# The gate tiles of attention in a two-block transformer kernel, with two of their three products merged and an addition on VectorE

## The reference

```python
(q_a, ..., k_i, w_i, gates) = split(h @ w_in)          # gates: 3 x 1024 columns
y_a = forgetting_attention(...)      # 6 heads
y_b = stick_breaking_attention(...)  # 5 heads
y_c = dsa_attention(...)             # 5 heads, keys picked by a top-64 of an index score
g_a, g_b, g_c = split(sigmoid(gates), 3)
merged = g_a * (y_a @ w_up_fox) + g_b * (y_b @ w_up_sb) + g_c * (y_c @ w_up_dsa)
return merged @ w_out
```

## Time and profile before

| what | us |
|---|---|
| median of 3 runs | 1989.26 (1988.9 to 1989.63) |
| the profiled execution's own time | 1987.53 |
| its span, first to last instruction | 1985.7 |
| outside the span | 1.83 |

### The profile page before, as it was taken

One profiled execution on the slowest core, in us unless ns is written; L12 is line 12 of the kernel. 1 busy time (PEld: TensorE's weight loads), 2 busy tenths in 40 slices (PEclk: granted clock), 3 DMA queues, 4 the chain that ended last, 5 costly groups with the idle time before them and its releaser, 6 DMA issues.

```text
span 1985.7 us, 32550 instructions
## 1 busy us (share of the span) xinstructions
PE 1928.3 (97%) x11892; PEld 1706.7 (86%) x11892; DVE 1529.5 (77%) x2655; ACT 1031.1 (52%) x1582; POOL 44.2 (2%) x80
## 2 busy tenths in 40 slices
PE   7999999999999999999999999999999999999998
PEld 6888899988888888899988888888788888897887
DVE  7988667679888988667678888785777778667776
ACT  5445555654455445545565446566544455555443
POOL 0000000000000000000000000000000000000000
PEclk9999999999999999999999999999999999999999
DMA  7885433348874876444347874542355554233553
GB/s 299 295 285 195 173 144 128 128 181 290 286 271 155 296 285 219 170 159 144 113 170 269 284 254 146 180 151 90 127 190 190 190 191 170 96 128 138 190 190 138
DMA packets 77285, 382.16 MB, mean 192 GB/s; under 512 B 9296, under 2 KB 9472, under 8 KB 55936
## 3 DMA queue, kind: packets, MB, share of 16 engines
q1 hardware_dynamic: 67392, 329.78, 45.6%
q0 software_dynamic: 9792, 51.00, 7.8%
HBM read 379.65 MB, written 1.10 MB: 192 GB/s over the span
## 4 chain that ended last, share of the span: by engine, by line
PE 86%; DVE 8%; ACT 3%; issue 2%; DMA 1%; SPq 0%; DVEq 0%; ACTq 0%
PE psum L671 20%; PE psum L588 16%; PE psum L589 16%; PE psum L590 16%; PE psum L676 11%; DVE weights_low_a L1470 1%; PE psum L902 1%; PE psum L692 1%; PE psum L839 1%; DVE merge_terms L1992 1%; PE psum L830 1%; ACT weights_high_a L1087 1%; PE psum L929 1%; PE psum L930 1%; DVE residual L1677 1%
## 5 line engine op out<-in xcount | busy, mean ns | idle before, releaser
L1470 DVE TENSOR_TENSOR weights_low_a<-raw_a,weights_high_a 128x2048 fp32r<-128x2048 f32 (+1 forms) x232 | 460.0, 1983 | 101.8 <-ACT weights_high_a L1087 99.4
L671 PE MATMUL psum<-h_high_low,weights_high_a 128*128 128x512 f32 x1760 | 424.0, 390 | 0.3 <-DVE weights_low_a L1470 0.3
L1087 ACT ACTIVATE weights_high_a<-raw_a 128x2048 fp32r<-128x2048 f32 (+1 forms) x232 | 385.8, 1663 | 62.8 <-PE psum L590 52.9
L671 PEld LDWEIGHTS psum<-h_high_low,weights_high_a 128*128 128x128 f32 x1760 | 329.9, 188 | 71.7 <-issue 1.9
L1470 DVE TENSOR_TENSOR weights_low_b<-raw_b,weights_high_b 128x1024 fp32r<-128x1024 f32 x224 | 273.3, 1220 | 50.1 <-ACT weights_high_b L1087 49.7
L1087 ACT ACTIVATE weights_high_b<-raw_b 128x1024 fp32r<-128x1024 f32 x224 | 235.5, 1052 | 96.4 <-PE psum L590 96.4
L1157 ACT ACTIVATE up_low_products<-psum 128x512 f32<-128x512 f32 (+1 forms) x146 | 74.0, 507 | 371.6 <-PE psum L676 364.6
L676 PEld LDWEIGHTS psum<-h_high_low,weights_low_a 128*128 128x128 f32 x1760 | 229.6, 191 | 11.0
L588 PE MATMUL psum<-weights_high_b,gated_high 128*128 128x512 f32 x608 | 238.4, 392 | 0.0
L589 PE MATMUL psum<-weights_low_b,gated_high 128*128 128x512 f32 x608 | 238.3, 392 | 0.0
L590 PE MATMUL psum<-weights_high_b,gated_low 128*128 128x512 f32 x608 | 236.5, 389 | 0.0
(11 more groups left out here) (306 smaller groups left out, 3233.9 us busy)
## 6 DMA issues: line engine op xcount, KB each, us to landing
ada_weights<-in_w_ada POOLq DMA_DIRECT2D x64, 768.0 KB, 5.9
raw_a<-in_w_ffn_a_a SPq DMA_DIRECT2D x44, 1024.0 KB, 7.0
raw_a<-in_w_ffn_b_a SPq DMA_DIRECT2D x44, 1024.0 KB, 7.5
raw_a<-in_w_ffn_a SPq DMA_DIRECT2D x64, 512.0 KB, 4.4
raw_b<-in_w_ffn_b SPq DMA_DIRECT2D x64, 512.0 KB, 3.3
raw_a<-in_w_proj_a SPq DMA_DIRECT2D x28, 1024.0 KB, 5.5
raw_a<-in_w_gate_a SPq DMA_DIRECT2D x26, 1024.0 KB, 4.9
raw_b<-in_w_ffn_a_b SPq DMA_DIRECT2D x44, 512.0 KB, 3.7
```

Of the source, the lines that this page charges most:

```text
L671: pe.matmul(ps[:, gates * p + m, :], whi[0][:, p, c:c + P], hboth[:, k, :, :].rearrange("p a b -> p (a b)"), start=k == 0, stop=False, ski ...
L1087: act.activation(whi[kind][:, p, 0:width], raw[kind][:, p, 0:width], ACT.Copy).then_inc(now().hi_ready[kind], 1)
L1470: dve.tensor_tensor(wlo[kind][:, p, 0:width], raw[kind][:, p, 0:width], whi[kind][:, p, 0:width].bitcast(F32), ALU.subtract).then_inc(lo_r ...
```

## The change

Gate tiles are formed as in the feed-forward: 8 products of 512 columns into the whole bank, then 8 of 256 columns of the low weights into its low half. The 6 query and key tiles of block one stay as they are. ACT now copies the high half, `ps[:, g % 2, SEQ:2 * SEQ]`, into the gate's place. DVE then adds the low half out of PSUM onto that copy (`gate_sum`), in its tick after the late half of a stick-breaking head and before the early work on scores. A new semaphore `gate_added` counts the sums. PE's tile g now waits for the sum of tile g - 2 in place of its copy, and the turning of the outputs and the tanh wait for the sums too.

```diff
             def gate_tile(l, blk, walk, g):
 
+                late = QK_LATE if blk == 1 else 0
                 if g >= 2:
-                    pe.wait_ge(now().gate_copied, g - 1)
+                    if g - 2 < late:
+                        pe.wait_ge(now().gate_copied, g - 1)
+                    else:
+                        pe.wait_ge(now().gate_added, g - 1 - late)
+                if g >= late:
+                    tiles = [walk.tiles[g * KD + k] for k in range(KD)]
+                    enter(l, blk, tiles[0])
+                    for k, tile in zip(range(KD), tiles):
+                        pe.matmul(ps[:, g % 2, :], weight(tile)[0], hboth[:, k, :, :].rearrange("p a b -> p (a b)"),
+                                  start=k == 0, stop=False, skip_group_check=True)
+                    for k, tile in zip(range(KD), tiles):
+                        m = pe.matmul(ps[:, g % 2, 0:SEQ], weight(tile)[1], hhi[:, k, :], start=False,
+                                      stop=k == KD - 1, skip_group_check=True)
+                    finish(m, k == KD - 1, tiles[-1])
+                    return
...
             def turn_y(blk, first, end):
 
                 if first == 0:
-                    pe.wait_ge(now().gate_copied, QK_LATE + 24 if blk == 1 else 16)
+                    pe.wait_ge(now().gate_added, 24 if blk == 1 else 16)
...
-                act.activation(out, ps[:, g % 2, 0:SEQ], ACT.Copy, scale=scale).then_inc(now().gate_copied, 1)
+                part = slice(0, SEQ) if g < late else slice(SEQ, 2 * SEQ)
+                act.activation(out, ps[:, g % 2, part], ACT.Copy, scale=scale).then_inc(now().gate_copied, 1)
...
-                act.wait_ge(now().gate_copied, (f + 1) * n + (QK_LATE if blk == 1 else 0))
+                act.wait_ge(now().gate_added, (f + 1) * n)
                 act.activation(g, g, ACT.Tanh, scale=0.5).then_inc(now().gates_ready, 1)
...
+            def gate_sum(blk, g):
+
+                late = QK_LATE if blk == 1 else 0
+                if g < late:
+                    return
+                gate = (g1 if blk == 1 else g2)[:, g - late, :]
+                dve.wait_ge(now().gate_copied, g + 1)
+                dve.tensor_tensor(gate, ps[:, g % 2, 0:SEQ], gate, ALU.add).then_inc(now().gate_added, 1)
+
             def ticks(l, blk, items, gates, n0):
                 for tick in range(len(items) + TURN_LAG + 2):
                     item_late(items, tick - 1)
+                    for g in gates_of(blk, tick):
+                        gate_sum(blk, g)
                     if tick < len(items) and items[tick]:
                         item_early(blk, items, tick)
```

More of the change, by code:

```diff
@@ L130, in __init__ @@
         self.gate_copied = one("gate_copied")
+        self.gate_added = one("gate_added")
         self.gates_ready = one("gates_ready")
```

## The result

The changed kernel takes 1999.79 us (median of 5 runs, 1999.04 to 2001.57) against 1989.26 (5 runs, 1988.90 to 1989.93): 1.0055 times as long, 95% interval 1.0044 to 1.0067, or +10.5 us. The profiled execution took 1999.26, its span is 1997.5. The forecast was slower by 5.2, with 2000 as the upper end of the range. The direction is right, and the forecast size is half of the measured one.

A forecast was written before the change was run, and what follows sets the result against it. PE was taken to bound the kernel (86% of the chain), with DVE nearly as busy in ticks 2 to 10 of block two. 2 x 2.2 + 2 x 0.4 = +5.2 us gave 1994.5 us, range 1986 to 2000.

The forecast's parts named there:

- The loop: Attention stages: early work (DVE), softmax and next gate copy (ACT), sum (DVE), next early work; block two +2.2 us a layer.
- the clock: PE's granted clock in the attention stages: the prediction had no term for its falls.
- block one: Block one's attention stage: +1.1 us at tile 10, then 19 tiles with 2.3 us of gain; taken as +0.4 a layer.
- block two after item 7: Block two's late ticks: from +2.2 us, 5 tiles give back 0.6, a late sum costs 0.5; taken as +2.2 a layer.
- The gain of a merged tile: PE, 80 gate tiles: each falls from 2.88 to 2.76 us, 9.6 us if all of it reaches the end.
- The rival of a tile no shorter: PE's gate tiles: a merged tile stays at 2.88 us, the sum is +7.8 us, 1997; chance 0.03.
- The cost of the sum: DVE: 80 additions of 128x256 out of PSUM, 0.42 us each, 27 to 34 us of DVE.
- the first rival: All four stages: sums hide in DVE's free time (26 us in block two's stage), PE's gain arrives; 1986 us, chance 0.14.
- my walk: Tick by tick lateness through each attention stage, PE's gain included: +2.2 us a layer in block two, +0.4 in block one.
- the loop costs more: Attention stages at the upper bounds, 2 x 4 + 2 x 1.1 = +10.2 us, 1999.5; late loads or longer sum waits; chance 0.11.

The follow-up runs named there:

- e2: Changed kernel without DVE's sums, PE waiting for the copy as before, the high by low product left out of each gate: 1983.24 us, ratio 0.9970.
- e1: Changed kernel with DVE's sum moved behind the early work of its tick instead of ahead of it: 1995.28 us, ratio 1.0038.
- e6: Changed kernel, but in block two ACT copies the whole bank to a scratch, PE waits only for that copy, DVE adds its halves: 2003.34 us.
- e5: Changed kernel with 8, 12, 10 and 8 filler products on PE ahead of four values products of block two: 2001.98 us, ratio 1.0064.
- e9: Changed kernel with 4, 7, 6 and 4 filler products on PE ahead of four values products of block two: 1995.90 us, ratio 1.0038.
- e7: Changed kernel with only 20 of 24 gate tiles of block one merged (not 6, 8, 16, 24), none of block two: 1986.18 us, ratio 0.9985.

## Why the prediction was half right

The loop was foreseen where it is, and nearly at its size up to item 7 of block two. Three terms failed: the clock, which was at nothing and made 3.2 us; block one, at +0.4 a layer and measured at +1.1; and block two after item 7, at 2.2 a layer in all and measured at 2.95. The gain of a merged tile was also taken a third too large.

**The merged tile: mis-sized.** "2.88 us" to "2.76 us", 9.6 us in all, came from the feed-forward, where these shapes stand. In the ticks it is 0.08 a tile and 6.3 us, and e2 measured 5.5. The distances that I called certain (0.11 to 0.13 a tile) were not: 512 columns take 0.231 there, not 0.226, and the first wide product behind other work takes 0.315 to the next start, where the first of 256 columns took 0.203. The rival of a tile no shorter is refuted all the same.

**The cost of the sum: right.** 80 additions at 0.424 us. (By the earlier trace rows DVE had 25 us free in block two's stage, not the 26 of the first rival. Nothing hangs on it.)

**The loop: right in place and in kind.** e1 opens it and block two loses 2 us of lateness. e6 takes away PE's wait instead, and nothing is gained. Each reading below has the stage's shift taken off (1.97 us in block two, 0.15 in block one). The values of item 7 were forecast 2.2 late; they start at 1341.15, 2.46 late. Tile 10 of block one was forecast to wait for a sum and to be 1.1 late; it does wait, and is 1.0 late. Tile 6 of block two was forecast to wait for the sum and to start 0.46 late; it starts at 1316.30, 0.49 late. But here the number is partly luck. These are tile 10, and then PE and DVE at tile 6:

```profile
301.61 2.12 PE L753 MATMUL psum<-h_high_low,weights_high_a 128*128 128x512 f32 x8 [0.98 <-DVE gates_one L1822]
...
1314.89 0.49 PE L846 MATMUL psum<-turned_two 64*128 64x128 f32 x4 [0.64 <-ACT turned_two L1307]
...
1316.30 2.11 PE L753 MATMUL psum<-h_high_low,weights_high_a 128*128 128x512 f32 x8
...
1315.82 0.76 DVE L1822 TENSOR_TENSOR gates_two<-psum,gates_two 128x256 f32<-128x256 f32 x2
```

PE's scores ahead of tile 6 already start 0.24 late (1312.68 before), after a wait for ACT's copy of turned tokens, which stands behind the late softmax and a high part. This is the same loop by a way that my walk did not have. Only the other 0.25 is the sum, which ends at about 1316.2.

**Block one after tile 10: wrong.** "After that come 19 tiles with 2.3 us of gain, at ticks with slack": 1.0 us of gain does come: the values at 356.54 start no later than before. But the turn of the loop at 357 to 361 us, shown above, sets PE back to 1.1 late at 361.53, whatever it had gained. Hence +1.1 a layer, the upper bound, not +0.4. A gain that is followed by one more turn of the loop is worth nothing.

**Block two after item 7: wrong.** "From here 5 tiles remain ... and they give back 0.6." The two long waits of PE that follow were there before, for ACT's turned probabilities and for DVE's outputs (1.32 and 0.99 us long). They are as long after:

```profile
1361.92 0.41 PE L944 MATMUL psum<-tokens_two,probs_turned_two 128*128 128x64 f32 x2 [1.33 <-ACT probs_turned_two L1318]
...
1362.65 3.59 PE L753 MATMUL psum<-h_high_low,weights_high_b 128*128 128x512 f32 x8
1366.09 1.10 PE L756 MATMUL psum<-h_high_low,weights_low_b 128*128 128x256 f32 x8
...
1370.46 0.41 PE L944 MATMUL psum<-tokens_two,probs_turned_two 128*128 128x64 f32 x2 [0.99 <-DVE y_two L1813]
```

So PE's pace does not decide there, and most of the tiles' gain falls into these waits. With the falls taken off, these two products are 2.3 and 2.2 late. From the 2.46 of item 7 some 0.25 is given back, not 0.6. Then 0.7 is lost at the last sum, where my walk had 0.5. The rows of DVE and PE there:

```profile
1374.62 0.42 DVE L1822 TENSOR_TENSOR gates_two<-psum,gates_two 128x256 f32<-128x256 f32 x1 [4.16 <-ACT gates_two L1330]
...
1375.36 1.22 DVE L1487 TENSOR_TENSOR weights_low_b<-raw_b,weights_high_b 128x1024 fp32r<-128x1024 f32 x1
...
1377.03 0.43 PE L944 MATMUL psum<-tokens_two,probs_turned_two 128*128 128x64 f32 x2 [0.32 <-DVE y_two L1813]
```

DVE stands 4.16 us in front of this sum, and the low part behind it, which ran in DVE's idle time before (at 1365.27), now runs ahead of the finishing of an output that PE waits for. The layer ends 2.95 late.

**The clock: not in the sum at all.** The granted clock was 1.00 in all four stages of before, and I took that for given, so this term stood at nothing without a reason. After, it falls twice to 0.5, which is the lower of its two levels, 1.2 GHz, in the profiled execution. The row of 3.59 us above shows a fall: the same eight products take 2.09 elsewhere. This is 3.2 us of the 11.7.

The Trainium skill ("TensorE: Matmul & The Clock Gate", section "Wait — 56ns, not 53.3ns?") gives a start every N/1.2 ns at the lower clock, 427 ns for 512 columns. The rows agree: (1366.09 - 1362.65) / 8 = 430 ns.

**The sum again.** Forecast 2 x 2.2 + 2 x 0.4 = 5.2. Measured in the profiled executions 2 x 2.95 + 1.22 + 1.03 = 8.15 for the waits, 3.19 for the falls, 0.39 outside the stages: 11.73. The medians are 10.5 apart. The rival "the loop costs more" had the nearest number, 1999.5. It had 0.11 of the chances. But it gave block two +4 a layer, for late loads or longer waits of each sum. In neither kernel does an engine wait for a load in the four stages, and block two's waits are 2.95 a layer. That its number comes near is luck: the falls fill the gap.

**What stays open.** Why the clock falls in one execution and not in another. In the stages it falls behind PE's waits of 1.3 to 1.7 us, and with fillers in these waits there is no fall in the profiled executions (e5, e9). But the waits alone don't settle it: the second layer of the kernel after has a wait of 1.50 and no fall, e7 has a fall behind the wait of 1.32 that the kernel before has too, without one, and e9 has none behind the wait of 3.10 us, where before has one. With one profile of each kernel I can't say how many falls a typical execution has in its stages; the clock over the whole span says only that nearly all executions have some, those of before too.

## What to carry to other kernels

When an eviction is split between two engines that work in order, look at what stands behind the second half on its engine, and whether the first half's engine waits for just that. If so, the two queues are locked in step, and the pace is the sum of both, however idle each is; put the sum behind the urgent work, or split only the tiles whose copy comes early anyway (e7). Look also at what else stands behind that second half: here a low part was pushed out of idle time into the path. A gain on the busiest engine counts only up to the next place where it waits for something else, so walk to the last such wait before adding gains up.

## What was not expected of the hardware

A fall of the granted clock in a stretch with PE busy 79 of 86 us, behind waits of no more than 1.6 us, at 1.55 us each. Idle time of PE can so cost twice, and with useless products in it this kernel was 3.6 to 3.9 us faster. The cost depends on the place: in the feed-forward stretches that hold the fall near 1611 us, kernels with it are 0.2 to 1.0 us longer than e5 and e9 without it. And the same products have different distances in different company: 512 columns every 0.227 us in the feed-forward and every 0.231 in the ticks.
